# Both tail blocks' second feed-forward matrix as seven block products

## The chip, the cores and the metric

The program runs on one core of one Trainium2 chip, in one launch. The metric is the device time of the whole program in microseconds (us), the median over the runs of one kernel. All data are float32.

## The reference, cut to what matters

The program computes a first block of two layers and then a second block of two layers on 256 tokens of width 1024. The change touches only the feed-forward part of the second block, which runs twice, once in each of its layers (called `A.` and `B.` in the kernel):

```python
ALPHA = (2 * DEPTH) ** 0.25          # DEPTH = 2; the residual is scaled by it

def sq_relu_mlp(x, w1, w2):          # x 256x1024, w1 1024x4096, w2 4096x1024
    return jnp.square(jax.nn.relu(x @ w1)) @ w2

x = layer_norm(ALPHA * x + sq_relu_mlp(x, mlp_w1[i], mlp_w2[i]), ln_ffn_g[i], ln_ffn_b[i])
```

The hidden activations are non-negative and 256x4096; the second product sums over 4096.

## The kernel before, in words

**Digits.** A float32 product is made of three single-pass products. Each operand is split into a high part (`hi`, a copy rounded to the type fp32r, made by ScalarE) and a low part (`lo`, the operand less its high part, made by VectorE), and TensorE sums `lo*hi + hi*lo + hi*hi` (`products`, line 562). A matmul whose operands are plain float32 is called native here.

**Tiles and ring.** Weights come in 2 MB tiles through a ring of three buffers. SyncE issues the load of the next tile into a buffer when TensorE has finished the tile that lay in it (`tile_used`, line 1886; TensorE signals it with the first matmul behind the tile, `tile_done` and `pay`, lines 484 and 458). The low part of a tile is written in place, over the tile (`w_lo`, line 330); the high part goes to two places of 2048 columns, `w_hi_tmp`/`w_hi_rows` and `w_hi_work`/`w_hi_big` in turn. The order of a block's tiles is ff1.0, ff1.1, ff2.0, ff1.2, ff2.1, ff1.3, ff2.2, ... ff1.7, ff2.6, ff2.7 (`_mlp_tiles`, line 117). So tile ff2.n lies in the buffer in which ff1.n lay, and ff1.(n+2) in the buffer of ff2.(n-1).

**The loop.** One turn of the loop is `ff1(n)` and `ff2(n-1)` (lines 621 and 668). `ff1(n)` makes 512 hidden columns as two units (f = 2n and 2n+1), each 48 matmuls of 256 columns into one of PSUM's banks 0 and 1 in turn. `ff2(n-1)` adds 512 rows of the second matrix to the output in banks 4 to 7: 48 matmuls of 512 columns. ScalarE (`act_mlp`, line 1140) and VectorE (`dve_mlp`, line 1167) follow in a fixed order written out by hand: ScalarE copies the high parts of the next tile and makes each unit's relu, square and high part (lines 1151, 1153, 1155), VectorE the low parts (lines 1107 and 1177). Every engine runs its instructions strictly in program order. Behind `ff2(7)` VectorE adds `ALPHA * x` (`add_mlp`, line 2601) and makes the layer norm.

A unit may start when its bank has been read (`wide_.saved`): with two banks this is the unit two before it.

Of the kernel before, what the change touches and what calls it, by code (L numbers as in the profile page):

```python
# [7 lines left out]
F32 = mybir.dt.float32  # L8
F32R = mybir.dt.float32r
ALU = mybir.AluOpType  # L10
ACT = mybir.ActivationFunctionType
# [136 lines left out]
SPLITS2 = ["sbo0", "sbo1"] + _mlp_tiles("A.") + ["dso0", "dso1"] + _mlp_tiles("B.")  # L148


def _places(splits):

    pairs = (("work", "big"), ("tmp", "rows"))
    late = {"in0": ("work", "zb"), "in1": ("tmp", "rows"), "in2": ("work", "scr"), "in3": ("tmp", "rows"),
            "in4": ("hT", "work"), "in5": ("z0", "big"), "in6": ("scr", "zb"), "in7": ("work", "hT"),
            "in8": ("zb", "scr"), "in9": ("work", "hT"), "in10": ("zb", "hT"),
            "up_nsa": ("mid", "tmp"), "up_ret": ("scr", "hT"),
            "out0": ("work", "zb"), "out1": ("mid", "tmp"),
            "gate0": ("tab0", "big"), "gate1": ("tmp", "rows"),
            "dso0": ("big", "big_a"), "dso1": ("big_b", "work")}  # L160
# [5 lines left out]
    places.update((name, mixed[name]) for name in splits if name in mixed)  # L166
    return places


# [104 lines left out]
def program(nc, ctx, I, out):  # L274
# [39 lines left out]
    def hid_slot(f):  # L314

        return f % (4 * HID_SLOTS)
# [13 lines left out]
    w_lo = [digits(f"w_lo{i}", f"ring{i}", 0, SLOT) for i in range(RING)]  # L330
    rows_t = rows[:, :].rearrange("p (t n) -> p t n", t=TT)

    gate_t = scr[:, 0:TT * D].rearrange("p (t n) -> p t n", t=TT)

    def part(lo, width, pattern=None, **sizes):
# [118 lines left out]
    def pe_kit(pe, st, wide_, aux_, tiles, splits, places):  # L454
# [134 lines left out]
        def mlp(pre, turns, between=None, second_token=None, between_at=3, last_turn=None):  # L589
# [31 lines left out]
            def ff1(n):  # L621
# [43 lines left out]
                            some(q, u, range(KT))  # L665
                tile_done()

            def ff2(n):
                lo, hi = next_split(f"{pre}ff2.{n}", 4, D)
                wait_split(f"{pre}ff2.{n}", 1)  # L670
                pe.wait_ge(hid_lo_ready.sem, st.at(hid_lo_ready, FB // 2 * mlp_nth(pre) + 2 * n + 2))
                for q in range(4):
                    t, c = divmod(q, 2)
                    for k in range(4):
                        last = n == 7 and k == 3
                        if n == 7 and q == between_at and k == 2 and between:
# [418 lines left out]
    def lower_split(st, eng, tiles, splits, name):  # L1095

        for h in range(2):
            lower_half(st, eng, tiles, splits, name, h)

    def lower_half(st, eng, tiles, splits, name, h):  # L1100

        n, nth = tiles.index(name), splits.index(name)
        signal, _ = lower_digits(name, splits)
        places, width = PLACES if splits is SPLITS else PLACES2, split_halves(name)
        c = slice(h * width, (h + 1) * width)
        eng.wait_ge(w_hi_ready.sem, st.at(w_hi_ready, 2 * nth + h + 1))
        eng.tensor_tensor(w_lo[n % RING][:, c], ring[n % RING][:, c], w_hi[places[name][h]][:, 0:width].bitcast(F32), ALU.subtract) \  # L1107
            .then_inc(st.up(signal), 1)

    def hidden_pairs(name):  # L1110

# [12 lines left out]
    def act_mlp_by_token(st, act, wide_, pre, tiles, splits, halves):  # L1124

        def save_rows(t):
            b, nth = wide_.next(f"{pre}f{t}")
            act.wait_ge(wide_.ready.sem, st.at(wide_.ready, nth))
            act.activation(hid_rows[t], b, ACT.Copy).then_inc(st.up(wide_.saved), 1)

        act_split(st, act, tiles, splits, f"{pre}ff1.1", halves)
        save_rows(0)
        save_rows(1)
        act_split(st, act, tiles, splits, f"{pre}ff2.0")
# [3 lines left out]
        act_mlp(st, act, wide_, pre, tiles, splits, 1)  # L1138

    def act_mlp(st, act, wide_, pre, tiles, splits, done=0):  # L1140

# [15 lines left out]
    def dve_mlp_by_token(st, dve, pre, tiles, splits):  # L1157

        lower_split(st, dve, tiles, splits, f"{pre}ff1.1")
        lower_split(st, dve, tiles, splits, f"{pre}ff2.0")  # L1160
# [1401 lines left out]
    def dve_tail(dve, st, head):  # L2562
        wide_, aux_ = wide.again(WIDE2), head.aux

        def tt(o, a, b, op):
            return dve.tensor_tensor(o, a, b, op)  # L2566
# [4 lines left out]
        def stt(o, a, s1, b, op0, op1):  # L2571
            return dve.scalar_tensor_tensor(out=o, in0=a, scalar=s1, in1=b, op0=op0, op1=op1)  # L2572
# [28 lines left out]
        def add_mlp(first, t, c):  # L2601
            n = 2 * t + c
            dve.wait_ge(ff2_ready.sem, st.at(ff2_ready, first + n + 1))
            xv = x[:, t, c * BANK:(c + 1) * BANK]
            stt(xv, xv, ALPHA, scores[:, n * BANK:(n + 1) * BANK], ALU.mult, ALU.add).then_inc(st.up(ff2_saved), 1)

        def layer_norm(n, add, between=None, turned_first=None):

# [559 lines left out]
```

## Time and profile before

| What | Value |
|---|---|
| median of 3 runs (lowest, highest) | 1469.02 us (1468.73, 1470.3) |
| span of the profiled execution | 1467.4 us |
| median less that span (what lies around it) | 1.6 us |
| PE busy | 1442.2 us, 98% of the span |
| DVE busy | 814.0 us, 55% |
| ACT busy | 730.8 us, 50% |
| DMA queue q1, share of 16 engines | 48.1% |

PE is TensorE's matmuls, PEld its weight loads, DVE VectorE, ACT ScalarE, SPq the queue of SyncE that issues the weight loads. The profile is of one execution; of its own time only the span, from the first instruction to the last, is shown, and the runs' median is 1.6 us above it. The loop of block A is at 1000.6 to 1171 us of the span, that of block B at 1290.4 to 1460 us. A matmul's duration in a row includes its way through the array, so neighbouring matmuls overlap: what one costs in a dense stretch is the distance of the starts.

### The profile page before, as it was taken

Reading aid. Unit: us, or ns where it says so; the run is one execution under the profiler, and the core shown is the slowest. Engines: PE = TensorE matmul, PEld = TensorE weight load, DVE = VectorE, ACT = ScalarE, POOL = GpSimd, SP = SyncE. Lnnn points to the kernel's source line nnn. Section 1 sums busy time; section 2 is a strip of 40 time slices with the busy share of each in tenths; the row PEclk is TensorE's granted clock in tenths of the full one; section 3 lists DMA queues with packets and bytes.
Section 4 is the critical chain, followed back from the end, with each engine's and each line's share of the span. In section 5 each row is a group of like instructions: output and inputs, shape, how many; then the busy total and the mean of one; then the engine's idle time right before and its main releaser. Section 6 shows DMA issues by size and latency. Waiting matters only on the chain.

```text
span 1467.4 us, 19978 instructions
## 1 busy us (share of the span) xinstructions
PE 1442.2 (98%) x8640; PEld 1231.4 (84%) x8640; DVE 814.0 (55%) x1010; ACT 730.8 (50%) x910; POOL 289.6 (20%) x109
## 2 busy tenths in 40 slices
PE   7999999999999999999999999999999999999998
PEld 5788889988877788888989788688998888888986
DVE  5337665454553364854444669875444557554445
ACT  4465635544455554654455366646544336264452
POOL 4598150000029694410000000000000004000000
PEclk9999999999999999999999999999999999999999
DMA  8833345654446543445566353215654453255451
GB/s 302 297 124 128 125 146 198 213 211 180 173 153 236 196 146 116 166 170 210 173 198 219 122 190 115 98 61 183 230 187 172 153 196 115 74 206 209 172 198 60
DMA packets 121222, 250.26 MB, mean 171 GB/s; under 512 B 15040, under 2 KB 27056, under 8 KB 121008
## 3 DMA queue, kind: packets, MB, share of 16 engines
q1 hardware_dynamic: 120872, 248.90, 48.1%
q8 instruction: 68, 1.11, 0.3%
q14 instruction: 18, 0.15, 0.0%
q10 hardware_dynamic: 264, 0.10, 0.0%
HBM read 247.94 MB, written 1.05 MB: 170 GB/s over the span
## 4 chain that ended last, share of the span: by engine, by line
PE 93%; DVE 4%; POOL 1%; issue 1%; ACT 1%; DMA 0%; DVEq 0%
PE psum L464 90%; PE psum L471 4%; DVE x L2572 1%; POOL w_lo L1107 1%; DVE big L2566 1%; DMA work<-in_norm_mix 0%; DVE rows L1379 0%; DVE w_lo L1107 0%; DVE tiny L2615 0%; DVE big L2572 0%; DVE ht_lo L1353 0%; DVE hT L1348 0%; DVE pT L2816 0%; DVE rows L2566 0%; DVE ht_lo L2566 0%
## 5 line engine op out<-in xcount | busy, mean ns | idle before, releaser
L464 PE MATMUL psum<-ht_hi,w_lo 128*128 128x256 f32 x960 | 269.2, 281 | 0.9 <-issue 0.6
L464 PE MATMUL psum<-w_lo,ht_hi 128*128 128x512 f32 (+1 forms) x576 | 222.5, 390 | 0.9 <-DVE w_lo L1107 0.9
L464 PE MATMUL psum<-w_lo,hid_hi 128*128 128x512 f32 x512 | 202.4, 395 | 0.0
L464 PEld LDWEIGHTS psum<-ht_hi,w_lo 128*128 128x128 f32 x960 | 179.7, 187 | 3.2 <-issue 2.0
L1087 ACT ACTIVATE w_hi_work<-ring 128x2048 fp32r<-128x2048 f32 x40 | 76.5, 1913 | 153.2 <-PE psum L464 150.5
L1107 DVE TENSOR_TENSOR w_lo<-ring,w_hi_work 128x2048 fp32r<-128x2048 f32 x29 | 66.5, 2292 | 129.9 <-ACT w_hi_work L1087 129.9
L1177 DVE TENSOR_TENSOR hid_lo<-work,hid_hi 128x512 fp32r<-128x512 f32 x60 | 41.5, 692 | 160.4 <-ACT hid_hi L1155 160.4
L464 PEld LDWEIGHTS psum<-w_lo,ht_hi 128*128 128x128 f32 x576 | 108.5, 189 | 22.5 <-DVE w_lo L1107 1.7
L464 PE MATMUL psum<-ht_lo,w_hi_rows 128*128 128x256 f32 x448 | 125.0, 279 | 0.0
L464 PE MATMUL psum<-ht_lo,w_hi_tmp 128*128 128x256 f32 x448 | 125.0, 279 | 0.0
L464 PE MATMUL psum<-ht_hi,w_hi_tmp 128*128 128x256 f32 x448 | 124.9, 279 | 0.0
L464 PE MATMUL psum<-ht_hi,w_hi_rows 128*128 128x256 f32 x448 | 124.4, 278 | 0.0
L464 PEld LDWEIGHTS psum<-w_lo,hid_hi 128*128 128x128 f32 x512 | 96.1, 188 | 21.7
L1107 POOL TENSOR_TENSOR w_lo<-ring,w_hi_work 128x2048 fp32r<-128x2048 f32 x12 | 57.5, 4795 | 255.2 <-ACT w_hi_work L1087 255.2
L1151 ACT ACTIVATE work<-psum 128x512 f32<-128x512 f32 x60 | 35.9, 598 | 142.3 <-PE psum L464 142.3
L1107 DVE TENSOR_TENSOR w_lo<-ring,w_hi_tmp 128x2048 fp32r<-128x2048 f32 x36 | 82.5, 2292 | 40.0 <-ACT w_hi_tmp L1087 40.0
L464 PE MATMUL psum<-hT,ring 128*128 128x256 f32 (+2 forms) x480 | 89.8, 346 | 0.0
L464 PE MATMUL psum<-w_hi_big,hid_lo 128*128 128x512 f32 x224 | 88.9, 397 | 0.0
L464 PE MATMUL psum<-w_hi_big,hid_hi 128*128 128x512 f32 x224 | 88.4, 395 | 0.0
L464 PE MATMUL psum<-w_hi_work,hid_hi 128*128 128x512 f32 x224 | 88.4, 395 | 0.0
L464 PE MATMUL psum<-w_hi_work,hid_lo 128*128 128x512 f32 x224 | 88.2, 394 | 0.0
L464 PEld LDWEIGHTS psum<-hT,ring 128*128 128x128 f32 (+1 forms) x480 | 78.2, 186 | 10.5 <-issue 2.4
(399 smaller groups left out, 3382.9 us busy)
## 6 DMA issues: line engine op xcount, KB each, us to landing
ring<-in_w_ff SPq DMA_DIRECT2D x32, 2048.0 KB, 7.9
ring<-in_mlp_w SPq DMA_DIRECT2D x32, 2048.0 KB, 8.4
ring<-in_w_in SPq DMA_DIRECT2D x19, 2048.0 KB, 8.1
ring<-in_w_out SPq DMA_DIRECT2D x4, 2048.0 KB, 8.1
ring<-in_w_ple_gate SPq DMA_DIRECT2D x4, 2048.0 KB, 8.0
ring<-in_sb_ssm_w_in SPq DMA_DIRECT2D x4, 2048.0 KB, 8.9
ring<-in_dsa_w_in SPq DMA_DIRECT2D x3, 2048.0 KB, 8.7
ring<-in_w_up_nsa SPq DMA_DIRECT2D x2, 2048.0 KB, 8.4
```

Source lines behind the costliest of these rows:

```text
L464: ins = pe.matmul(o, lhsT, rhs, start=start, stop=stop)
L471: ins = pe.transpose(o, in_, ident[0:n, 0:n])
L1087: act.activation(w_hi[place][:, 0:width], ring[n % RING][:, h * width:(h + 1) * width], ACT.Copy) \
L1107: eng.tensor_tensor(w_lo[n % RING][:, c], ring[n % RING][:, c], w_hi[places[name][h]][:, 0:width].bitcast(F32), ALU.subtract) \
L1151: act.activation(h, b, ACT.Relu).then_inc(st.up(wide_.saved), 1)
L1177: dve.tensor_tensor(lo, h, hi.bitcast(F32), ALU.subtract).then_inc(st.up(hid_lo_ready), 1)
L2566: return dve.tensor_tensor(o, a, b, op)
L2572: return dve.scalar_tensor_tensor(out=o, in0=a, scalar=s1, in1=b, op0=op0, op1=op1)
```

## The change

In the tail blocks (`SEVEN = ("A.", "B.")`) `ff2(0)` to `ff2(6)` are replaced. A tile's 256x512 hidden values and 512x1024 weights are cut in two by two blocks: tokens in halves, the 512 summed rows in halves (of each pair of 128 rows the first or the second, `v`), output columns in halves. The eight block products are replaced by seven, of 128 tokens x 256 rows x 512 columns each, with sums of blocks as operands (the scheme with four sums on either side and seven sums behind). Each product has a PSUM bank (1 to 7) of its own over all seven tiles; the units of `ff1` have bank 0 alone. Five products are made by digits (two rows of 128 each, three matmuls: 6 matmuls a tile), two, into banks 2 and 6, natively in float32 (2 matmuls a tile). The sums, their low parts and the last sums into `x` are VectorE's, the high parts ScalarE's. `ff2(7)` stays as it is, but adds onto the products in banks 4 to 6, and onto an empty bank 7 once VectorE has read it; `ALPHA` is applied in `dve_seven_products`, and `add_mlp` only adds. The high parts of ff1.2 to ff1.7 are split by columns (one half per unit) and all use `tmp`/`rows`; those of ff2.0 to ff2.6 use `work`/`big`. The core of the diff:

```diff
+            def ff1_unit(n, q, w):
+                lo, hi = w
+                wait_split(f"{pre}ff1.{n}", q)
+                _, nth = wide_.next(f"{pre}f{2 * n + q}")
+                pe.wait_ge(wide_.saved.sem, st.at(wide_.saved, nth + 1))
+                ... 48 products matmuls into bank[0]
+            def seven_first(n, lo):
+                m, s = seventh(pre, n), 4 * (n % 2)
+                pe.wait_ge(form_hi.sem, st.at(form_hi, DIGIT_FORMS * m + 1))
+                pe.wait_ge(hid_lo_ready.sem, ...2 * n + 2))
+                for o, v in ((bank[4], 1), (bank[1], 0)):
+                    for u in range(2):
+                        f = s + 2 * u + v
+                        mm(o, hid_lo[:, f, 0:P], col_hi[:, u, v, :], n == 0 and u == 0, False)
+                        mm(o, hid_hi[:, f, 0:P], col_hi[:, u, v, :], False, False, ...)
+            def seven_rest(n, lo):
+                pe.wait_ge(form_lo.sem, st.at(form_lo, DIGIT_FORMS * m + 1))
+                ... hid_hi * low columns, 4 matmuls, banks 4 and 1
+                pe.wait_ge(s_low.sem, st.at(s_low, m + 1))
+                pe.wait_ge(form_lo.sem, st.at(form_lo, DIGIT_FORMS * m + 2))
+                by_digits(bank[5], 2, right_hi[:, :, 1, :], w[:, :, 1, BANK:D], False, None)
+                by_digits(bank[7], 0, right_hi[:, :, 0, :], w[:, :, 0, BANK:D], final, form_used)
+                pe.wait_ge(form_lo.sem, st.at(form_lo, DIGIT_FORMS * m + 3))
+                by_digits(bank[3], 1, t_hi[0], t_lo[0], final, form_used)
+                ... bank[2]: s_form(sums_, 3, u) * t_sum[1], native, 2 matmuls
+                ... bank[6]: hid_f[:, s + 2 * u + 1, P:S] * t_sum[2], native, 2 matmuls
-            for n in range(1, 8):
-                ff1(n)
-                ff2(n - 1)
+            ... ff1(1); seven_first(0, lo); seven_rest(0, lo)
+                for n in range(2, LAST + 1):          # LAST = 7
+                    w = next_columns(f"{pre}ff1.{n}")
+                    ff1_unit(n, 0, w)
+                    lo = seven_open(n - 1)
+                    seven_first(n - 1, lo)
+                    ff1_unit(n, 1, w)
+                    tile_done()
+                    seven_rest(n - 1, lo)
+                    tile_done()
             ff2(7)
+    def act_column_forms(st, act, tiles, pre, n):
+        act.wait_ge(tile_in[at % RING].sem, ...)       # tile ff2.n has landed
+        act.activation(col_hi, blocks(ring[at % RING][:, :])[:, :, :, 0:BANK], ACT.Copy)...
+    def act_right_forms(st, act, tiles, pre, n):
+        act.wait_ge(t_summed.sem, st.at(t_summed, 4 * m + 2))
+        act.activation(right_hi, blocks(ring[at % RING][:, :])[:, :, :, BANK:D], ACT.Copy)...
+        act.activation(t_hi[0], t_sum[0], ACT.Copy)...
+    def act_hidden_forms(st, act, pre, n):
+        act.wait_ge(s_summed.sem, ...); act.activation(s_hi[n % 2], s_sum[n % 2][:, 0:S_WIDTH], ACT.Copy)...
+    def act_mlp_seven(...):                            # hidden(f): relu, square, high part of unit f
+        for n in range(2, LAST):
+            hidden(2 * n)
+            act_split(st, act, tiles, splits, f"{pre}ff1.{n + 1}", (0,))
+            act_column_forms(st, act, tiles, pre, n)
+            hidden(2 * n + 1)
+            act_split(st, act, tiles, splits, f"{pre}ff1.{n + 1}", (1,))
+            act_hidden_forms(st, act, pre, n)
+            act_right_forms(st, act, tiles, pre, n)
+        hidden(2 * LAST); act_split(... ff2.7, (0,)); hidden(2 * LAST + 1); act_split(... ff2.7, (1,))
+    def dve_mlp_seven(st, dve, pre, tiles, splits):
+        for n in range(1, LAST):
+            lower_columns(st, dve, tiles, splits, f"{pre}ff1.{n + 1}", 0)   # 128x2048
+            dve_hidden_sums(st, dve, pre, n)           # 4 sums of 128x256
+            dve_hidden_first(st, dve, pre, n)          # 128x512
+            lower_columns(st, dve, tiles, splits, f"{pre}ff1.{n + 1}", 1)   # 128x2048
+            dve_form_sums(st, dve, tiles, pre, n)      # 4 sums of 128x1024, each waits for the last
+            dve_form_lows(st, dve, tiles, pre, n, range(2))                 # 2 of 128x2048
+            dve_hidden_sums_low(st, dve, pre, n)       # 128x768
+            dve_form_lows(st, dve, tiles, pre, n, range(2, DIGIT_FORMS))    # 128x1024
+        ... low parts of ff2.7 and of units 14, 15
+    def dve_seven_products(st, dve, pre):              # behind dve_mlp_seven
+        dve.wait_ge(seven_done.sem, ...)
+        ... 4 scaled sums, 1 copy, 5 sums, all 128x512; the last signals seven_read
             def ff2(n):
                 for q in range(4):
+                    if pre in SEVEN and q == 3:
+                        pe.wait_ge(seven_read.sem, ...)
```

For n = 1 both halves of ff1.2 are split ahead of the hidden sums; for n = 0 the forms stand ahead of the units' relu.

## Rows read from the trace of the kernel before

**Rows 1.** The page: the chain that ended last, by engine.
```profile
PE 93%; DVE 4%; POOL 1%; issue 1%; ACT 1%; DMA 0%; DVEq 0%
```
**Rows 2.** Windows of ff1(3), ff2(2): PE, PEld, DVE, ACT, POOL busy, clock, DMA, GB/s.
```profile
1046.40:1057.80 11.40, 11.40 (x98) 11.36 (x97) 5.18 (x3) 5.58 (x5) 0.00 (x0) 1.00 0.52 185
1057.80:1068.90 11.10, 11.10 (x49) 8.95 (x49) 5.19 (x3) 5.48 (x5) 0.00 (x0) 1.00 0.52 189
```
**Rows 3.** Timeline of PE in that turn (start, us; line; out<-in; shape).
```profile
1046.44 0.28 PE L464 MATMUL psum<-ht_hi,w_lo 128*128 128x256 f32 x1
...
1057.73 0.40 PE L464 MATMUL psum<-w_hi_work,hid_lo 128*128 128x512 f32 x1
...
1068.92 0.28 PE L464 MATMUL psum<-ht_hi,w_lo 128*128 128x256 f32 x1
```
**Rows 4.** Timeline of PE around four native matmuls (8 records).
```profile
403.17 3.59 PE L464 MATMUL psum<-big,pT 128*128 128x512 f32 x8
406.20 0.80 PE L464 MATMUL psum<-w_hi_tab,ht_lo 128*128 128x512 f32 x1
406.84 0.40 PE L464 MATMUL psum<-w_lo,ht_hi 128*128 128x512 f32 x1
```
**Rows 5.** Timeline of SPq, and the load's time from issue to landing.
```profile
1058.16 0.37 SPq L1899 DMA_DIRECT2D ring<-in_mlp_w  x1
...
ring<-in_mlp_w SPq DMA_DIRECT2D x1, 2048.0 KB, 7.8
```
**Rows 6.** Timeline of ACT in that turn (in brackets: idle before, releaser).
```profile
1046.81 1.92 ACT L1087 ACTIVATE w_hi_work<-ring 128x2048 fp32r<-128x2048 f32 x1 [5.83 <-PE psum L464]
1048.63 1.90 ACT L1087 ACTIVATE w_hi_big<-ring 128x2048 fp32r<-128x2048 f32 x1
...
1057.93 0.60 ACT L1151 ACTIVATE work<-psum 128x512 f32<-128x512 f32 x1 [3.72 <-PE psum L464]
...
1059.76 1.90 ACT L1087 ACTIVATE w_hi_tmp<-ring 128x2048 fp32r<-128x2048 f32 x1
```
**Rows 7.** Timeline of DVE in that turn.
```profile
1059.89 0.69 DVE L1177 TENSOR_TENSOR hid_lo<-work,hid_hi 128x512 fp32r<-128x512 f32 x1 [4.96 <-ACT hid_hi L1155]
1061.70 2.29 DVE L1107 TENSOR_TENSOR w_lo<-ring,w_hi_tmp 128x2048 fp32r<-128x2048 f32 x1 [1.11 <-ACT w_hi_tmp L1087]
1063.91 2.28 DVE L1107 TENSOR_TENSOR w_lo<-ring,w_hi_rows 128x2048 fp32r<-128x2048 f32 x1
```
**Rows 8.** Groups by line and shape: busy us, mean ns, idle before.
```profile
L1379 DVE TENSOR_TENSOR big<-big 128x1024 f32<-128x1024 f32 x4 | 4.9, 1220 | 0.1
L2566 DVE TENSOR_TENSOR big<-big 128x256 f32<-128x256 f32 x8 | 3.0, 422 | 0.1
L1287 ACT ACTIVATE big<-big 128x1024 f32<-128x1024 f32 x2 | 2.1, 1040 | 0.0
```
**Rows 9.** Windows around a gap of PE (columns as rows 2), PE's timeline behind it.
```profile
933.10:935.60 2.50, 0.02 (x1) 0.00 (x0) 2.47 (x4) 2.50 (x2) 0.00 (x0) 0.92 0.97 279
935.60:939.00 3.40, 3.20 (x8) 2.15 (x9) 1.16 (x3) 0.43 (x1) 0.00 (x0) 0.55 1.01 384
...
935.80 3.38 PE L464 MATMUL psum<-tmp,const 128*128 128x384 f32 x8 [2.68 <-DVE rows L2566]
```
**Rows 10.** Timeline of PE early in the program.
```profile
20.73 0.63 PE L464 MATMUL psum<-w_hi_work,ht_hi 128*128 128x512 f32 x1
21.16 0.63 PE L464 MATMUL psum<-w_hi_work,ht_lo 128*128 128x512 f32 x1
```
**Rows 11.** Timeline of DVE at the end of block B, last layer norm.
```profile
1454.53 0.69 DVE L2572 SCALAR_TENSOR_TENSOR x<-x,psum 128x512 f32<-128x512 f32 x1 [1.30 <-PE psum L464]
1455.25 0.69 DVE L2615 BATCH_NORM_STATS2 tiny<-x 128x6 f32<-128x512 f32 x1
...
1456.23 2.87 DVE L2572 SCALAR_TENSOR_TENSOR x<-x,tiny,const 128x512 f32<-128x512 f32 x4
...
1462.01 2.87 DVE L2572 SCALAR_TENSOR_TENSOR x<-x,tiny,const 128x512 f32<-128x512 f32 x4
```

More of the change, by code:

```diff
@@ L147, with _seven_tiles, _by_columns @@
 SPLITS = [f"in{c}" for c in range(N_IN)] + ["up_nsa", "up_ret"] + ["out0", "out1"] + _mlp_tiles("") + ["gate0", "gate1"]
-SPLITS2 = ["sbo0", "sbo1"] + _mlp_tiles("A.") + ["dso0", "dso1"] + _mlp_tiles("B.")
+LAST = 7
+SEVEN = ("A.", "B.")
+DIGIT_SUMS = 1
+DIGIT_FORMS = 2 + DIGIT_SUMS
+def _seven_tiles(pre):
+    return [f"{pre}ff2.{n}" for n in range(LAST)] if pre in SEVEN else []
+def _by_columns(name):
+    pre, _, kind = name.rpartition("ff1.")
+    return pre in SEVEN and kind.isdigit() and int(kind) >= 2
+SPLITS2 = ["sbo0", "sbo1"] + [n for n in _mlp_tiles("A.") if n not in _seven_tiles("A.")]
+SPLITS2 += ["dso0", "dso1"] + [n for n in _mlp_tiles("B.") if n not in _seven_tiles("B.")]
 def _places(splits):
@@ L166, in _places @@
     places.update((name, mixed[name]) for name in splits if name in mixed)
+    for pre in SEVEN:
+        if f"{pre}ff1.0" in splits:
+            places.update((f"{pre}ff1.{n}", pairs[1]) for n in range(1, LAST + 1))
+            places.update((name, pairs[0]) for name in _seven_tiles(pre))
+            places[f"{pre}ff2.{LAST}"] = pairs[1]
     return places
@@ L666, in ff1 @@
                 tile_done()
+            def ff1_unit(n, q, w):
[4 more added lines that the diff above has]
+                for u in range(2):
+                    c = slice((2 * q + u) * P, (2 * q + u + 1) * P)
+                    for k in range(KT):
+                        last = k == KT - 1
+                        products(bank[0][:, u * S:(u + 1) * S], hi(k, c), lo[:, k, c], ht_hi[:, k, :], ht_lo[:, k, :],
+                                 k == 0, last, wide_.ready if last and u == 1 else None)
@@ L688, in mlp @@
                 ff1(0)
-            for n in range(1, 8):
-                ff1(n)
-                ff2(n - 1)
+            if pre in SEVEN:
+                ff1(1)
+                lo = seven_open(0)
+                seven_first(0, lo)
+                seven_rest(0, lo)
+                tile_done()
[7 more added lines that the diff above has]
+                    seven_rest(n - 1, lo)
+                    tile_done()
+            else:
+                for n in range(1, 8):
+                    ff1(n)
+                    ff2(n - 1)
             ff2(7)
@@ new lines, in act_right_forms @@
+    def act_right_forms(st, act, tiles, pre, n):
+        at, m = tiles.index(f"{pre}ff2.{n}"), seventh(pre, n)
+        form_free(st, act, tiles, pre, n, 2)
+        act.wait_ge(t_summed.sem, st.at(t_summed, 4 * m + 2))
+        act.activation(right_hi, blocks(ring[at % RING][:, :])[:, :, :, BANK:D], ACT.Copy).then_inc(st.up(form_hi), 1)
+        act.activation(t_hi[0], t_sum[0], ACT.Copy).then_inc(st.up(form_hi), 1)
+        if DIGIT_SUMS > 1:
+            act.wait_ge(t_summed.sem, st.at(t_summed, 4 * m + 3))
+            act.activation(t_hi[1], t_sum[1], ACT.Copy).then_inc(st.up(form_hi), 1)
@@ new lines, in act_hidden_forms, with act_mlp_seven, hidden @@
+    def act_hidden_forms(st, act, pre, n):
+        act.wait_ge(s_summed.sem, st.at(s_summed, seventh(pre, n) + 1))
+        act.activation(s_hi[n % 2], s_sum[n % 2][:, 0:S_WIDTH], ACT.Copy).then_inc(st.up(s_high), 1)
+    def act_mlp_seven(st, act, wide_, pre, tiles, splits):
+        def hidden(f):
+            turn, nth = wide_.next(f"{pre}f{f}")
+            b = turn if f < 4 else bank[0]
+            act.wait_ge(wide_.ready.sem, st.at(wide_.ready, nth))
+            at = hid_slot(2 * f)
+            hi, h = (v[:, at:at + 2, :].rearrange("p f t -> p (f t)") for v in (hid_hi, hid_f))
+            act.activation(h, b, ACT.Relu).then_inc(st.up(wide_.saved), 1)
+            act.wait_ge(st.last.sem, st.reached())
+            act.activation(h, h, ACT.Square).then_inc(st.up(act_step), 1)
+            act.wait_ge(st.last.sem, st.reached())
+            act.activation(hi, h, ACT.Copy).then_inc(st.up(hid_hi_ready), 1)
+        hidden(2)
+        act_hidden_forms(st, act, pre, 0)
+        hidden(3)
+        act_split(st, act, tiles, splits, f"{pre}ff1.2")
+        act_column_forms(st, act, tiles, pre, 1)
+        act_hidden_forms(st, act, pre, 1)
+        act_right_forms(st, act, tiles, pre, 1)
+        for n in range(2, LAST):
[6 more added lines that the diff above has]
+            act_right_forms(st, act, tiles, pre, n)
+        hidden(2 * LAST)
+        act_split(st, act, tiles, splits, f"{pre}ff2.{LAST}", (0,))
+        hidden(2 * LAST + 1)
+        act_split(st, act, tiles, splits, f"{pre}ff2.{LAST}", (1,))
@@ new lines, in dve_form_sums @@
+    def dve_form_sums(st, dve, tiles, pre, n):
+        at = tiles.index(f"{pre}ff2.{n}")
+        w = blocks(ring[at % RING][:, :])
+        b11, b12, b21, b22 = (w[:, :, v, c * BANK:(c + 1) * BANK] for v in range(2) for c in range(2))
+        sums_ = ((t_sum[0], b22, b12), (b12, b12, b11), (t_sum[1], b22, b12), (t_sum[2], b21, t_sum[1]))
+        dve.wait_ge(tile_in[at % RING].sem, st.at(tile_in[at % RING], 16 * (at // RING + 1)))
+        for (o, a, b), nth in zip(sums_, (3, None, 4, 5)):
+            if nth:
+                form_free(st, dve, tiles, pre, n, nth)
+            dve.tensor_tensor(o, a, b, ALU.subtract).then_inc(st.up(t_summed), 1)
+            dve.wait_ge(st.last.sem, st.reached())
@@ new lines, in dve_form_lows @@
+    def dve_form_lows(st, dve, tiles, pre, n, which):
+        at, m = tiles.index(f"{pre}ff2.{n}"), seventh(pre, n)
+        w, lo = blocks(ring[at % RING][:, :]), blocks(w_lo[at % RING][:, :])
+        forms = [(lo[:, :, :, 0:BANK], w[:, :, :, 0:BANK], col_hi), (lo[:, :, :, BANK:D], w[:, :, :, BANK:D], right_hi)]
+        forms += [(t_lo[i], t_sum[i], t_hi[i]) for i in range(DIGIT_SUMS)]
+        for i in which:
+            low, v, hi = forms[i]
+            dve.wait_ge(form_hi.sem, st.at(form_hi, DIGIT_FORMS * m + i + 1))
+            dve.tensor_tensor(low, v, hi.bitcast(F32), ALU.subtract).then_inc(st.up(form_lo), 1)
@@ L1133, in act_mlp_by_token @@
         save_rows(1)
-        act_split(st, act, tiles, splits, f"{pre}ff2.0")
+        if pre in SEVEN:
+            act_column_forms(st, act, tiles, pre, 0)
+            act_right_forms(st, act, tiles, pre, 0)
+        else:
+            act_split(st, act, tiles, splits, f"{pre}ff2.0")
         for t in range(TT):
```

161 lines of the change are left out of this document (156 added, 5 removed).

## The prediction, made before the change was run

> **What bounds the kernel now.** First the chain that ended last: TensorE makes up 93% of it [rows 1], so the span is a stream of matmuls, and only what lengthens, shortens or interrupts this stream counts. Then the windows of one turn of the loop: PE is busy for all of both, at the full clock, while DVE works 10.4 and ACT 11.1 of 22.5 us [rows 2]. PE's timeline gives the price of the work by the distance of starts [rows 3]: ff1(n), 96 matmuls of 256 columns, takes 1057.73 - 1046.44 = 11.29 us (0.118 each), ff2(n-1), 48 of 512 columns, 1068.92 - 1057.73 = 11.19 us (0.233 each); a turn takes 22.48 us. Last the timelines of ACT, DVE and SPq in this turn, for how far behind TensorE the other engines run: the load of ff2.3 is issued 0.43 us after ff1(3) ends and lands 7.8 us later [rows 3, 5], and yet nobody waits for it, since ACT's next copy waits for TensorE alone, 5.83 us [rows 6]. That is the slack which the change spends.
>
> **TensorE's own work.** A tile of ff2.0 to ff2.6 had 48 matmuls. Now it has 5 x 6 = 30 by digits, 30 x 0.233 = 6.99 us, and 4 native ones. Four native 128x512 matmuls (8 records) begin at 403.17; the second single-pass matmul behind them begins at 406.84, less one distance 0.233 is 406.61, so 3.44 us in all, 0.86 each [rows 4]. Together 10.43 us for 11.19: 0.76 saved a tile, 10.6 us over 14 tiles, if nobody waits. A turn has 21.72 us of work for TensorE.
>
> **Who waits.** Four things in the code form a loop. (1) ff2.n is loaded into the buffer of ff1.n, so not before unit 2n+1 is done. This is as before. (2) ScalarE now has `act_column_forms(n)`, which waits for that landing, ahead of `hidden(2n+1)`. Queued behind the waiting copy are the relu of unit 2n+1 and all else of ScalarE. (3) The units have bank 0 alone, so unit 2n+2 waits for the relu of unit 2n+1, and unit 2n+3 for that of 2n+2; before, each had one unit of slack. (4) ScalarE reaches `hidden(2n+2)` only behind `act_right_forms(n)`, which waits for VectorE's second form sum, and VectorE comes to that only behind the hidden sums, which need unit 2n+1's high part. So from the end of unit 2n+1 to the end of unit 2n+3, one turn later:
> - to the issue 0.43, landing 7.8 [rows 3, 5];
> - column copy, 2048 wide: start to start 1.82 [rows 6];
> - relu, square, high part, to DVE's start: 1057.93 to 1059.89, 1.96 [rows 6, 7];
> - four hidden sums of 256, each about 0.42 and 0.02 for its wait: 1.76 [rows 8];
> - low part of 512: 0.69, less the 0.08 by which two of DVE overlap (2.29 long, starts 2.21 apart): 0.61; low columns of ff1.(n+1): 2.21 [rows 7];
> - two form sums of 1024: 1.22 each, with the wait between them 2.5 [rows 8];
> - ScalarE's right half 1.82 [rows 6], `t_hi` 1.04 less the overlap, 0.96 [rows 8], relu 0.60 and its signal 0.05 [rows 6];
> - unit 2n+3, 48 x 0.118 = 5.65 [rows 3].
>
> The sum is 28.17; for the hand-overs left out I add 0.1 and take 28.3 us. The rest of DVE's turn (two more form sums, low parts of 2048 twice, 1024 and 768, 2048 for the next tile) fits in beside this: all of DVE's is about 18.7 us, all of ACT's about 13.3. TensorE idles 28.3 - 21.7 = 6.6 us a turn: ahead of unit 2n+2, since the relu of 2n+1 has read bank 0 only 0.43 + 7.8 + 1.82 + 0.65 = 10.7 us after the unit and `seven_rest` lasts 8.57, 2.1 us; ahead of unit 2n+3 4.4 us. A turn costs 28.3 - 22.48 = 5.8 us more. This holds for unit 5 to unit 15, five turns: +29.1 us a block.
>
> **The ends of each block.** From unit 3 to unit 5 no landing is in the way yet (ScalarE has relu 3 ahead of the column copy of ff2.1), but two `seven_first` lie in this turn: 10.43 + 5.65 + 1.86 + 5.65 = 23.6, and the hidden sums and their low part stand between the second token's hidden values and TensorE, where one low part of 0.7 stood; I take 1.0 for it, so 24.6 for 22.48, +2.1. Behind unit 15 the landing of ff2.7 (8.23), a split (1.82), relu, square and high part of unit 15 (1.84, three of ACT back to back), the second split (1.90) and its low part (2.33) end at 16.1 us, while `seven_rest(6)` covers 8.6: TensorE idles 7.5 us. Then VectorE makes ten sums of 512 for the products, each priced as the 0.69 of its low part [rows 7], 7.0, to 23.1, and two tokens' adds and norm: four of 0.72, an aggregation of 0.25, 2.87 for the norm, 6.0 each [rows 11], to 35.1. The fourth quarter of ff2(7) starts at 16.1 + 8.4 = 24.5, after `seven_read`, and ends at 27.3, so VectorE is last here. Before, the second quarter ended at about 1454.4 [rows 11], so unit 15 at 1454.4 - 5.6 - 11.2 = 1437.6, and VectorE at 1462.01 + 2.87 = 1464.9: 27.3 us. So +7.8. In block A the first token's norm, for which the next stage waits, is late by the same.
>
> **The clock.** Where PE idled 2.68 us, the granted clock fell to 0.5 at about the gap's end and stayed there for (0.08 x 2.5 + 0.45 x 3.4) / 0.5 = 3.5 us [rows 9]: 1.2 for 2.4 GHz. At that level starts of 512-column matmuls are 0.43 us apart [rows 10] against 0.233, so a fall costs at most 3.5 x (1 - 0.233/0.43) = 1.6 us, and less where part of it lies in the gap. The new 4.4 us gap stands right ahead of a unit that is on the loop's path. From nothing to 1.6, I take 1.2, being nearest to that row: five turns, two blocks, 12 us. A fall behind the 2.1 us gap would only eat into the 4.4 us gap, and one behind the 7.5 us gap is covered by VectorE.
>
> The Trainium skill says the same against this change: by TensorE: Matmul & The Clock Gate, "Loop structure matters more than you think", a long DMA wait between bursts of matmuls makes each burst start cold. By that rule the clock is paid for in every turn; were it not so, the sum would lack its 12 us. The one mid-kernel gap of this trace agrees.
>
> **The sum.** A block: 2.1 + 29.1 + 7.8 = 39.0; two: 78; clock 12; together +90. The profiled execution's span of 1467.4 becomes 1557.4; the runs' median lay 1.6 above the span, so 1559 us.
>
> **The rivals.**
> - *The clock stays up.* Same loop without the 12 us: 1547. For it: only one gap in the trace shows a fall in mid-kernel, and weight loads and short bursts go on in each turn. Against it: 4.4 us is longer than that gap. 20%.
> - *The clock stays down.* If the three gaps of a turn's work leave the clock low for most of it, both units (11.3) and part of the tile run at 0.43 for 0.233; the 4.4 us slack ahead of the odd unit then covers the even one, and the odd unit on the path costs up to 4.8 instead of 1.2: 10 x 3.6 = 36 more, 1595; half of that, 1577, where it comes and goes. 10%.
> - *Less waiting than the loop says.* A transfer is hidden better than I see (landing earlier in the turn, or the form sums ready before the relu): 25 us a turn, 33 less, 1526. 6%.
> - *Faster: the arithmetic alone counts.* One mechanism: TensorE's stream stays dense, because the waits of ScalarE's queue end inside `seven_rest` and `seven_first`. The price is then -10.6 us, 1458 us. It decides where the loop above takes under 21.7 us, 6.6 less than worked out; 100% PE in the windows of before, 5.83 us of ACT's slack and a landing that nobody awaits speak for it; against it, that the landing alone (8.23) and the relu behind it outlast the 8.57 us of `seven_rest`, whatever the rest costs. 4%.
>
> My forecast has the other 60%. The 8-in-10 range takes in the first rival and half of the second: 1536 to 1582, which is also the forecast with 27.2 to 31.8 us a turn (clock and all) where I take 29.5. A change of under 0.2%, 3 us, can't be told from none here; faster by more 4%, within it 1%, slower 95%.
>
> **What would show it.** In the windows of the loop PE is busy about 0.77 and a turn lasts 28 to 30 us. ACT's column copy (`w_hi_work<-ring`) is released by the DMA of `in_mlp_w`, its right copy (`w_hi_big<-ring`) by DVE, DVE's hidden sums by ACT, and PE's first matmul of each unit by ACT's relu. Ahead of ff2(7) PE waits some 7.5 us for a low part. The clock falls about once a turn. Native matmuls cost 0.86. I am wrong if the column copy doesn't end a wait for the landing, or if PE's gaps sum to under 4 us a turn.

## The result and the profile after

The changed kernel takes 1544.85 us, median of 4 runs (1542.31 to 1546.61); the kernel before, on the same chip, 1468.88 (1467.16 to 1470.3). The ratio is 1.0522, 95% interval 1.0507 to 1.0537: 76 us slower. The forecast was 1559, range 1536 to 1582. In later series some executions of several kernels, the one before included, are 13 to 16 us longer by one wait in the first block, which no kernel here changes (last section); they widen some intervals, and where such a kernel is compared, the median of the other executions stands beside it.

| | before | after |
|---|---|---|
| span of the profiled execution | 1467.4 us | 1544.0 us |
| PE busy | 1442.2 (98%) | 1457.6 (94%) |
| DVE busy | 814.0 (55%) | 933.0 (60%) |
| ACT busy | 730.8 (50%) | 753.5 (49%) |

The chain that ended last, by engine and by line, which answers to [rows 1]:

```profile
PE 77%; DVE 9%; ACT 6%; DMA 5%; issue 1%; POOL 1%; DVEq 0%; ACTq 0%
```

PE made up 93% of it, and DMA, ACT and DVE together 5%. Now those three hold 20%: the chain leaves TensorE once a turn. The waits between 1000 and 1250 us, block A (us in total, times, longest), name the hand-overs:

```profile
ACT w_hi_work L1282 <- DMA ring<-in_mlp_w: 62.8, 6, 13.2
DVE work L1364 <- ACT hid_hi L1312: 56.9, 5, 12.3
PEld psum L515 <- issue: 49.1, 64, 4.5
PE psum L515 <- ACT work L1308: 29.3, 10, 4.1
ACT w_hi_big L1289 <- DVE ring L1344: 25.4, 6, 4.6
```

L1282 is the column copy (the high part of a ff2 tile's left columns), L1308 the relu, L1364 the first hidden sum, L1289 the right copy (the high part of its right columns), L1344 the form sums (of a tile's blocks). All but the third line (TensorE's weight loads, idle with its matmuls) are the four releases that the prediction named. The ring of them can be read once round. PE's timeline, from one odd unit to the next:

```profile
1090.05 0.36 PE L515 MATMUL psum<-ht_hi,w_lo 128*128 128x256 f32 x1 [2.59 <-ACT work L1308]
...
1095.78 1.10 PE L515 MATMUL psum<-w_lo,hid_hi 128*128 128x512 f32 x4
...
1106.63 0.36 PE L515 MATMUL psum<-ht_hi,w_lo 128*128 128x256 f32 x1 [2.11 <-ACT work L1308]
...
1118.49 0.36 PE L515 MATMUL psum<-ht_hi,w_lo 128*128 128x256 f32 x1 [4.12 <-ACT work L1308]
```

The same stretch in the chain of waits (start, us, what; where two instructions overlap, a start is up to 0.1 us later than in a timeline):

```profile
1090.05 6.14 PE psum L515 x49
...
1096.20 7.87 DMA ring<-in_mlp_w
...
1104.09 1.91 ACT w_hi_work L1282
1106.00 0.49 ACT work L1308
...
1107.18 0.64 ACT hid_hi L1312
...
1107.85 0.42 DVE work L1364
...
1110.23 2.28 DVE w_lo L1262
1112.51 1.15 DVE big L1344
...
1113.68 1.24 DVE ring L1344
```

and ACT's timeline where the chain comes back to it:

```profile
1104.09 1.91 ACT L1282 ACTIVATE w_hi_work<-ring 128x2048 fp32r<-128x2048 f32 x1 [11.06 <-DMA ring<-in_mlp_w]
...
1115.00 1.91 ACT L1289 ACTIVATE w_hi_big<-ring 128x2048 fp32r<-128x2048 f32 x1 [4.59 <-DVE ring L1344]
1116.82 1.04 ACT L1290 ACTIVATE t_hi<-big 128x1024 fp32r<-128x1024 f32 x1
```

The odd unit is done at 1095.78 (the matmuls of `seven_rest` start), load issued at 1096.20, landed after 7.87 us, column copy from 1104.09, relu at 1105.91, hidden sums from 1107.85, low columns from 1110.23, form sums from 1112.43, right copy from 1115.00, `t_hi`, relu, and the next odd unit at 1118.49. From odd unit to odd unit (1090.05 to 1118.49) that is 28.44 us; the prediction's sum was 28.17, taken as 28.3.

The clock comes on top. Windows (columns as [rows 2]; the clock is the third column from the end) of a unit behind a 2.11 us gap and of the start of one behind a 4.12 us gap:

```profile
1106.60:1112.40 5.80, 5.77 (x49) 5.80 (x50) 4.39 (x6) 3.78 (x4) 0.00 (x0) 1.00 0.76 243
1118.40:1122.40 4.00, 3.91 (x21) 3.94 (x22) 4.00 (x3) 3.04 (x3) 0.00 (x0) 0.62 0.00 0
```

The second unit lasts from 1118.49 to 1125.74, 7.25 us, where the one at 1090.05 took 5.73: this fall to half, 1.2 GHz, costs 1.5 us. The right copy (L1289) starts at 1027.1 for n = 1 and at 1175.6 for n = 6, so five turns last 148.5 us, 29.7 each; in block B (1356.94 to 1503.24) 29.3. The prediction had 29.5 with the clock.

### The profile page after: what moved, and what is told of

Read it like the earlier page. It is cut to its first block, busy times and chain, and to the rows that moved or that the text cites. A ratio compares the mean times of both kernels' runs of the same rounds, so it can differ in the third digit from the quotient of the medians.

```text
span 1544.0 us, 19971 instructions
## 1 busy us (share of the span) xinstructions
PE 1457.6 (94%) x8500; PEld 1223.3 (79%) x8500; DVE 933.0 (60%) x1156; ACT 753.5 (49%) x938; POOL 289.3 (19%) x109
## 4 chain that ended last, share of the span: by engine, by line
PE 77%; DVE 9%; ACT 6%; DMA 5%; issue 1%; POOL 1%; DVEq 0%; ACTq 0%
PE psum L515 74%; DMA ring<-in_mlp_w 5%; PE psum L522 3%; DVE w_lo L1262 1%; ACT w_hi_big L1289 1%; ACT w_hi_work L1282 1%; DVE ring L1344 1%; DVE big L1344 1%; DVE x L2916 1%; ACT work L1308 1%; ACT t_hi L1290 1%; POOL w_lo L1255 1%; DVE big L2910 1%; ACT hid_hi L1312 0%; ACT work L1310 0%
## 5 line engine op out<-in xcount | busy, mean ns | idle before, releaser
L515 PE MATMUL psum<-ht_hi,w_lo 128*128 128x256 f32 x960 | 280.1, 292 | 58.1 <-ACT work L1308 57.1
L515 PEld LDWEIGHTS psum<-ht_hi,w_lo 128*128 128x128 f32 x960 | 188.5, 196 | 72.5 <-issue 71.7
L515 PE MATMUL psum<-w_lo,hid_hi 128*128 128x512 f32 x344 | 129.7, 397 | 0.0
L515 PEld LDWEIGHTS psum<-ht_lo,w_hi_rows 128*128 128x128 f32 x448 | 91.7, 205 | 0.1
L515 PEld LDWEIGHTS psum<-ht_hi,w_hi_rows 128*128 128x128 f32 x448 | 90.1, 201 | 0.0
L1255 POOL TENSOR_TENSOR w_lo<-ring,w_hi_big 128x2048 fp32r<-128x2048 f32 x3 | 13.7, 4565 | 401.2 <-DVE work L2910 401.2
L515 PEld LDWEIGHTS psum<-ht_lo,w_hi_tmp 128*128 128x128 f32 x448 | 87.4, 195 | 1.1 <-issue 0.5
L1282 ACT ACTIVATE w_hi_work<-ring 128x2048 fp32r<-128x2048 f32 x14 | 26.7, 1910 | 124.7 <-DMA ring<-in_mlp_w 124.7
L515 PEld LDWEIGHTS psum<-ht_hi,w_hi_tmp 128*128 128x128 f32 x448 | 86.2, 192 | 0.0
L1364 DVE TENSOR_TENSOR work<-work 128x256 f32<-128x256 f32 x14 | 5.9, 424 | 118.6 <-ACT hid_hi L1312 111.7
L515 PEld LDWEIGHTS psum<-w_lo,hid_hi 128*128 128x128 f32 x344 | 63.9, 188 | 14.2 <-issue 0.5
L1521 DVE TENSOR_TENSOR hid_lo<-work,hid_hi 128x512 fp32r<-128x512 f32 x32 | 22.1, 691 | 83.6 <-ACT hid_hi L1495 83.6
```

What stands on the lines that cost most here:

```text
L515: ins = pe.matmul(o, lhsT, rhs, start=start, stop=stop)
L1282: act.activation(col_hi, blocks(ring[at % RING][:, :])[:, :, :, 0:BANK], ACT.Copy).then_inc(st.up(form_hi), 1)
```

## The experiments

Each started from the changed kernel ("after" below) unless it says otherwise. Times are medians; in brackets the ratio to the kernel before, run beside it, with its 95% interval.

**e1: the relu ahead of the column copy.** In `act_mlp_seven`:

```diff
-            act_column_forms(st, act, tiles, pre, n)
             hidden(2 * n + 1)
+            act_column_forms(st, act, tiles, pre, n)
             act_split(st, act, tiles, splits, f"{pre}ff1.{n + 1}", (1,))
```

> ScalarE makes unit 2n+1's relu, square and high part ahead of the column copy that waits for ff2.n's landing; the second half of ff1.(n+1) and all else stay behind that copy. Theory (the loop of four steps): unit 2n+2 no longer waits, but VectorE's form sums still stand behind the low columns of ff1.(n+1), whose high part comes behind the column copy: 8.23 landing, 1.82 and 1.90 two copies of ACT, 2.21 low columns, 2.5 form sums, 1.82 and 0.96 right copy and t_hi, 0.65 relu, 5.65 unit = 25.8 us a turn for 28.3, the gap of about 4 us ahead of the odd unit stays and with it the clock falls. 10 turns: 25 us less than the changed kernel, 1520. Rival 1, only the landing counts and the rest has slack: turns fall to 21.7, near 1467. Rival 2, the copy's place is harmless since the right copy is what sets the turn: no change, 1545.

Measured 1521.68 us (1.0369, 1.0353 to 1.0384). Waits from 1050 to 1180 us, and windows of the start of an odd unit and of the turn before it:

```profile
DVE w_lo L1262 <- ACT w_hi_rows L1225: 36.7, 5, 7.4
PE psum L515 <- ACT work L1308: 19.8, 5, 4.1
```
```profile
1084.10:1087.30 3.20, 3.15 (x15) 3.18 (x16) 3.20 (x2) 3.00 (x3) 0.00 (x0) 0.50 0.02 5
1056.70:1084.10 27.40, 23.49 (x134) 19.90 (x134) 18.11 (x16) 12.73 (x13) 0.00 (x0) 0.94 0.43 154
```

The gap ahead of even units is gone; one of 3.9 to 4.1 us ahead of each odd unit is left, and the clock is at half behind each. A turn is 27.4 us, the 25.8 worked out and 1.6 more, which one fall of the clock (1.5 in the unit above) nearly makes up. The theory holds and both rivals fall: the copy's place costs 2.3 us a turn (29.7 to 27.4), no more, because the form sums still stand behind a half of ff1.(n+1) that is split after the landing: VectorE waits up to 7.4 us for its high part (L1225) ahead of its low columns (L1262).

**e2: the next unit's relu ahead of the right copy.**

```diff
+        hidden(4)
         for n in range(2, LAST):
-            hidden(2 * n)
             ...
             act_hidden_forms(st, act, pre, n)
+            hidden(2 * n + 2)
             act_right_forms(st, act, tiles, pre, n)
-        hidden(2 * LAST)
```

> ScalarE makes unit 2n+2's relu, square and high part ahead of the right copy and t_hi of ff2.n, where it stood behind them; the column copy keeps its place ahead of unit 2n+1's relu. Theory: VectorE's form sums leave the loop, the landing stays: 8.23, 1.82, 0.65, unit 5.65, seven_first 1.86, unit 5.65 = 23.9 us a turn. The 4.4 us gap ahead of odd units goes, the 2.1 us one ahead of even units stays, on the path now. If a gap of 2 us doesn't bring the clock down: 10 turns by 5.6 less than 29.5, 1489; if it does, 1.2 a turn more, 1501. Rival, VectorE's own order sets the turn whatever ScalarE does: over 1535.

Measured 1496.18 us (1.0218, 1.0174 to 1.0261), 1496.0 by the three executions without the long wait. PE's waits from 1055 to 1165 us:

```profile
PE psum L515 <- DVE s_lo L1389: 6.0, 4, 1.9
PE psum L515 <- ACT work L1308: 3.4, 2, 2.0
```

Column copies start at 1060.2 (n = 2) and 1157.9 (n = 6): 24.4 us a turn for the 23.9 worked out. Three of these turns are 24.0 to 24.2, one, behind a fall of the clock at 1079, is 25.6. So the time lies between my two prices, 1489 and 1501, since the clock fell behind some gaps near 2 us and not behind others. What I had not put down: the gap is mostly not ahead of the even unit but inside `seven_rest`, where PE waits for the hidden sums' low part (`s_lo`). It hardly costs more, as turns of 24.0 to 24.2 for 23.9 say: by the sum, the relu would have held the next unit for the same 2 us.

**e3: the relu and the half of ff1.(n+1) ahead of the column copy.**

```diff
-            act_column_forms(st, act, tiles, pre, n)
             hidden(2 * n + 1)
             act_split(st, act, tiles, splits, f"{pre}ff1.{n + 1}", (1,))
+            act_column_forms(st, act, tiles, pre, n)
```

> ScalarE makes unit 2n+1's relu, square and high part and the second half of ff1.(n+1) ahead of the column copy that waits for the landing. Theory: hidden sums and low columns are done (6.5 us behind the unit) before the tile lands (8.23), form sums 10.7, right copy and t_hi 13.8, unit 2n+2 ends at 14.2 and its relu is not late. Nothing in the loop outlasts TensorE's own 21.7 us a turn; no gaps, no clock falls: 10 turns by 7.8 less, 1467. Rival 1, the clock falls come from something else than the gaps: 1467 + 12 = 1479. Rival 2, my 21.7 is short, since the native products or the fourth product wait for VectorE's form sums and low parts inside seven_rest: over 1480, with PE waiting for DVE there.

Measured 1464.18 us (0.9976, 0.9965 to 0.9987). The window from the right copy of n = 1 to that of n = 6:

```profile
1026.40:1134.80 108.40, 108.40 (x671) 92.04 (x670) 90.56 (x76) 64.45 (x60) 0.00 (x0) 1.00 0.57 203
```

Five turns in 108.4 us, 21.7 each, as TensorE's own work says; PE without a gap, the clock at 1.00. Two moved lines take 80 us off, and the kernel is 0.24% faster than the one before, clear of noise but small. The column copy still waits for the landing, 4.2 to 4.5 us a turn, but nothing that the chain needs in that time is queued behind it. Both rivals fall: in the loop no clock falls without the gaps, and PE waits for no low part. From the end of unit 5 to that of unit 15 the ten turns of both blocks last 217.3 us for 224.9 before, 7.6 less; the turn from unit 3 to unit 5 still lasts 24.35 for 22.49 in each block, 3.7 more. The balance of 3.9 less is near the 2.9 by which its time lies below the kernel before (1464.2 for 1467.1).

**e5: the load of ff2.7 made late.** In `sp_tail`, for `A.ff2.7` and `B.ff2.7` alone:

```diff
-            sp.wait_ge(tile_used.sem, where.value(tile_used, n + 1))
+            late = name in ("A.ff2.7", "B.ff2.7")
+            sp.wait_ge(tile_used.sem, where.value(tile_used, n + 2 if late else n + 1))
```

> The load of ff2.7 waits for one tile more (ff1.7), as my prediction had it. Theory: in the changed kernel ff2.7 lies in the buffer of ff2.5 and had landed before unit 15 was done, so the 7.5 us of waiting that I put ahead of ff2(7) never was; made to wait here, it should appear in both blocks: ff2(7) starts 16.1 us behind unit 15 instead of 8.2, and each block's last norm ends 35.1 us behind unit 15 for 26.6 to 29.3 now, 14 us in all: 1559, my forecast. Rival, the end of a block is set by VectorE's ten sums and norms alone, or the landing hides: under 1550.

Measured 1558.77 us (1.0622, 1.0606 to 1.0638), 13.9 above after. PE's timeline at the start of ff2(7) in block A:

```profile
1199.65 0.77 PE L515 MATMUL psum<-w_hi_tmp,hid_lo 128*128 128x512 f32 x1 [7.62 <-DVE w_lo L1255]
```

The wait that I had forecast for the changed kernel, 7.5 us for a low part, is here and 7.62 long. In the changed kernel it doesn't exist. The time is that of my forecast; that they meet to 0.2 us is luck, since other terms were off by some us (next section).

**e8: the gap filled.** 24 matmuls of `ht_hi` with itself, added into bank 7 where they falsify a product, between `seven_first` and the odd unit:

```diff
                     seven_first(n - 1, lo)
+                    for k in range(24):
+                        mm(bank[7][:, 0:S], ht_hi[:, k % KT, 0:P], ht_hi[:, k % KT, :], False, False)
                     ff1_unit(n, 1, w)
```

> The changed kernel with 24 more matmuls of 256 columns (2.8 us), nobody's input, ahead of each odd unit from 5 to 15, in the gap of 4.1 us in which TensorE waits for the relu; they add products into bank 7 that don't belong there. Theory: the turn stays 28.3 us by the loop, the longest gap becomes some 1.5 us, the clock no longer falls behind it, and the 1.2 to 1.6 us a turn that the falls cost go: 1545 less 12, 1533. Rival 1, the clock falls for another reason (the load of a tile, the smaller gap ahead of the even unit): 1545. Rival 2, TensorE's gap is no slack, and the matmuls lengthen the path: 1545 + 10 to 28.

Measured 1536.99 us (1.0455, 1.0374 to 1.0537), 1534.9 by three of four. The window of four turns, from the column copy of n = 2 to that of n = 6:

```profile
1047.90:1161.60 113.70, 101.19 (x632) 86.64 (x632) 72.06 (x60) 50.64 (x48) 0.00 (x0) 0.98 0.41 148
```

A turn is 28.4 us, the bare loop, where after has 29.7: 2.8 us of work added a turn, and each turn 1.3 shorter. No odd unit, ahead of which the gap is now at most 1.3 us, has a fall any more, so those falls come from the long gap. The total gains 8 to 10 us for the 12 put down: unit 5 of each block had no gap to hide the filler (its turn, from column copy to column copy, is 27.0 for 23.9 in block A and 25.4 for 22.7 in block B), and at five of the ten gaps ahead of even units, these five of 1.9 to 2.2 us, the clock still fell.

**e4: block A alone.** `SEVEN = ("A.",)`. Block B then has the old products, but its last add leaves out the factor `ALPHA` on the residual.

> The changed kernel with the seven products in block A alone; block B is as before. Theory: the cost is one block's loop, and nothing carries over from A to B: block A's last norm is 39 us late as in the changed kernel, block B runs as before, 1468 + 39 = 1507. Rival: part of the cost is outside the two loops (a clock that stays down, loads shifted against the rest of the program), so that half the change costs clearly more or less than half of 76: under 1500 or over 1515.

Measured 1506.13 us (1.0226, 1.0159 to 1.0292), from 1501.0 to 1510.6: 37.9 above the kernel before at 1468.2 (without the long wait), half of 76, with a scatter of some 5 us to either side. It fits two separate loops, and the rival (under 1500 or over 1515) falls.

**e6, on top of e3: six products by digits.** `DIGIT_SUMS = 2`.

> On top of e3 (no waits in the loop) the sixth product, into bank 2, is made by digits too: 6 matmuls of 0.233 us for 2 native ones of 0.86, 1.40 for 1.72, 0.32 us a tile; ScalarE gets a copy of 1.0 us and VectorE a low part of 1.2 us a tile more. Theory: with the loop free, TensorE's own work sets the turn, 21.4 us for 21.7, and 14 tiles save 4.5: 1460. Rival 1, VectorE's 1.2 us more lies on the path inside seven_rest: PE waits there for a low part, and the time is that of e3 or above it, 1464 to 1475. Rival 2, a native matmul costs no more than three single-pass ones (0.70): 1464.

Measured 1462.64 us (0.9921, 0.9881 to 0.9961); without the long wait 1462.4 for 1468.2 before, so 5.8 below it where e3 was 2.9. Four turns from the column copy of n = 2:

```profile
1061.50:1147.20 85.70, 85.70 (x546) 75.27 (x544) 78.03 (x64) 55.60 (x52) 0.00 (x0) 1.00 0.55 197
```

21.43 us a turn; e3's same four turns (1045.20 to 1132.27) are 21.77 each. 0.34 saved, 0.32 expected, which sets a native matmul at 0.86 or 0.87, not 0.70. But the gain is 2.9 (1.8 if the two times themselves are compared), not 4.5: the turn from the end of unit 3 to that of unit 5 grew from 24.35 to 25.4 us in each block. PE waits there for a relu, which it doesn't in e3:

```profile
PE psum L515 <- ACT work L1308: 0.8, 1, 0.8
```

So a relu of ScalarE's comes late there; that its extra copy is what delays it is argued, not tested. Half a miss.

**e7, on top of e3: early sums.** In `dve_seven_products`:

```diff
-        dve.wait_ge(seven_done.sem, st.at(seven_done, mlp_nth(pre) + 1))
+        used = 4 * seventh(pre, LAST - 1)
+        dve.wait_ge(form_used.sem, st.at(form_used, used + 2))   # bank 7 (and 1) done
         ...
+        dve.tensor_copy(y_sum, bank[1])...                       # moved up, ahead of the next wait
+        dve.wait_ge(form_used.sem, st.at(form_used, used + 3))   # ahead of the sum with bank 3
         ...
+        dve.wait_ge(form_used.sem, st.at(form_used, used + 4))   # ahead of the sum with bank 2
```

> On top of e3 the sums behind the seven products each wait only for the product that they read, where all waited for the last product, which they don't read. Theory: VectorE's 2.5 us of waiting for PE at the end of each block goes, and the norms come 2.3 us sooner in both blocks, until the last quarter of ff2(7) sets them: 1464.2 less 4.6, 1459.6. Rival, the norm waits for ff2(7) anyway: 1464, VectorE's wait only moves to its first add behind ff2(7).

Measured 1460.18 us (0.9948, 0.9909 to 0.9988); without the long wait 1459.7 for 1468.2, 8.5 below where e3 was 2.9: 5.6 gained, 4.6 expected. VectorE at the end of block A, first e3, then e7:

```profile
1149.54 2.29 DVE L1255 TENSOR_TENSOR w_lo<-ring,w_hi_rows 128x2048 fp32r<-128x2048 f32 x1 [1.11 <-ACT w_hi_rows L1235]
1154.35 2.48 DVE L1423 SCALAR_TENSOR_TENSOR x<-x,psum 128x512 f32<-128x512 f32 x4 [2.52 <-PE psum L515]
```
```profile
1147.19 2.29 DVE L1255 TENSOR_TENSOR w_lo<-ring,w_hi_rows 128x2048 fp32r<-128x2048 f32 x1 [1.11 <-ACT w_hi_rows L1235]
1149.40 1.87 DVE L1423 SCALAR_TENSOR_TENSOR x<-x,psum 128x512 f32<-128x512 f32 x3
```

The 2.52 us wait is gone.

**e9: e3, e6 and e7 together.**

> The order of ScalarE of e3, six products by digits of e6 and the early sums of e7 together. Theory: the three are on different stretches, so the gains add: 1464.2 less 4.5 less 4.6, 1455. Rival, VectorE at some 20 us of a 21.4 us turn is near its own bound and falls behind, and the sum is less than 5 us.

Measured 1457.86 us (0.9917, 0.9877 to 0.9957); without the long wait 1456.6 for 1468.2, 11.6 below the kernel before, where the parts sum to 2.9 + 2.9 + 5.6 = 11.4. It is the best version here, 0.8% faster than the kernel before, and the rival of VectorE at its bound falls. Its PE is busy for 98% of the span, as before the change: nearly all that is left is TensorE's own stream.

## Why the prediction was right, and where not

**The mechanism** was right, step by step: the four releases stand in the waits of the profile after, and undoing them one at a time gave the turns that the sum gives without them: 27.4 for 25.8 and a fall of the clock (e1), 24.0 to 24.2 for 23.9 (e2), 21.7 for 21.7 (e3). The step that mattered most is (2): from n = 2 on a wait of 11 to 13 us ahead of everything else in ScalarE's queue. Before, ScalarE's copies waited for TensorE and not for a landing [rows 6]; the transfer took 7.8 us then [rows 5] and 7.9 now. Only what stood behind it changed.

**TensorE's own work** was right. The timeline of PE in block A's last tile, four native matmuls and what follows:

```profile
1192.26 3.60 PE L515 MATMUL psum<-big,work 128*128 128x512 f32 x8
1195.29 0.80 PE L515 MATMUL psum<-w_hi_tmp,hid_lo 128*128 128x512 f32 x1
1195.93 0.40 PE L515 MATMUL psum<-w_lo,hid_hi 128*128 128x512 f32 x1
```

Read as [rows 4] were: 1195.93 - 0.233 - 1192.26 = 3.44, 0.86 each. The gain of 0.76 a tile is real and shows as soon as nobody waits (e3).

**The turns** were right. From the end of one odd unit to the end of the next, the bounds of the sum (in block A 1037.65, 1067.56, 1095.78, 1125.74, 1156.48, 1187.11), three of the ten turns last 28.2 to 28.4 us (28.3 forecast): in them the odd unit runs at the full clock. In the other seven, 29.8 to 30.7, 30.2 on average, the clock falls at the odd unit, in or behind a gap of 4.12 us. All ten last 296.7 us for 224.9 before, 71.8 more; forecast 10 x (5.8 + 1.2) = 70.

**The clock** holds two errors that nearly cancel, which is luck: ten falls at 1.2 us were put down, seven at 1.9 were paid. There are ten, one a turn. But three came at the gap of 1.9 to 2.2 us ahead of the even unit (block A's at 1078.2): they make that unit slower, so that the gap ahead of the odd one is 2.6 us for 4.1, and no fall came there. So they are free, as the prediction said of such a fall. The price is higher than 1.2: four paid falls hold the clock at half for some 3.4 us, as in [rows 9], and make their turn 1.5 to 1.7 us longer than 28.3, since they lie almost wholly inside the odd unit. The other three (two of them in block A) hold it for some 6.8 us and cost 2.2 to 2.4. One of these starts inside the gap ahead of the unit at 1148.54 and ends in that unit at 1153.4:

```profile
1146.50:1147.00 0.50, 0.00 (x0) 0.00 (x0) 0.50 (x1) 0.50 (x2) 0.00 (x0) 0.65 0.00 0
...
1152.50:1153.00 0.50, 0.50 (x5) 0.50 (x4) 0.50 (x2) 0.00 (x0) 0.00 (x0) 0.50 0.00 0
```

By the page that the prediction drew on, the Trainium skill's TensorE: Matmul & The Clock Gate, "Loop structure matters more than you think", a long wait for a transfer ahead of matmuls makes TensorE run them at its lower clock. The trace agrees in direction, in seven of ten odd units. e8 shows that the price goes with the long gap, 1.3 us a turn over block A's last four.

**The signs.** The four releases and the price of a native matmul came as named. PE is busy for 0.80 of block A's five turns (120.1 of 149.4 us) and 0.81 of block B's (119.5 of 147.3) for the 0.77 named, since its gaps sum to 5.9 and 5.6 us a turn for 6.6: the falls in even units take from them, and matmuls at half clock count as busy. The wait of 7.5 us ahead of ff2(7) did not come.

**The rival "the clock stays up"** (1547) lies nearer to the measured 1544.85 than the forecast does. By the number alone it would have won; the trace rules it out, since the clock is at half in every turn. The number is near for another reason, the next term. **The rival "the clock stays down"** fell: outside these ten stretches the clock was at full speed in both loops.

**The ends of each block** hold the mis-sized term: +7.8 us forecast for each, about 0 measured. SP's, ACT's and PE's timelines at the end of block A:

```profile
1167.64 0.37 SPq L2243 DMA_DIRECT2D ring<-in_mlp_w  x1
```
```profile
1180.19 1.90 ACT L1235 ACTIVATE w_hi_tmp<-ring 128x2048 fp32r<-128x2048 f32 x1
1187.31 0.60 ACT L1308 ACTIVATE work<-psum 128x512 f32<-128x512 f32 x1 [5.22 <-PE psum L515]
...
1189.14 1.90 ACT L1235 ACTIVATE w_hi_rows<-ring 128x2048 fp32r<-128x2048 f32 x1
```
```profile
1187.11 1.10 PE L515 MATMUL psum<-w_lo,hid_hi 128*128 128x512 f32 x4
```

The load of ff2.7 is issued at 1167.64, 19.5 us before unit 15 is done at 1187.11, and its first half is copied at 1180.19 without a wait. The sum has it issued 0.43 us behind unit 15, by the rule that ff2.n lies in the buffer of ff1.n, which also stands in the description of the kernel before. That holds for n from 1 to 6 only. The order of tiles ends ..., ff2.5, ff1.7, ff2.6, ff2.7: three back from ff2.7 is ff2.5, not ff1.7. So `seven_rest(6)` and ff2(7) follow each other with no gap, VectorE's ten sums run beside ff2(7), and its last norm ends at 1541.56 in block B, 26.8 us behind unit 15 (1514.75), where it was 27.3 before [rows 11] and 35.1 forecast. In block A it is 29.2 for 28.8. e5 shows it: give the load the release that I had in mind, and both the 7.5 us wait and the 1559 us appear.

The balance of the profiled span, by the sum's own bounds (ends of units): +76.6, of it turns 71.8 (forecast 70), the turns from unit 3 to unit 5 3.7 (24.35 for 22.49 in each block; forecast 4.2), ends 0.0 (forecast 15.6), and 1.1 that I did not place (forecast nothing). So but for the ends the forecast would have been 1543, for 1544.85 measured.

**Less waiting** (1526) and **faster** (1458) fell as forecasts, but e3 meets the second one's condition, a loop that fits in 21.7 us, and PE's stream is dense there. It takes 1464 and not 1458, since the turns from unit 3 to unit 5 still cost 3.7 us; e9 reaches 1458 by two more changes.

## What to carry to other kernels

An algorithm with fewer matmuls pays only while TensorE's stream stays dense: here the loop cost 5.8 us a turn, without the clock, where the arithmetic saved 0.76. Add up, in program order, the whole ring from one release to the same release a turn later, with every engine's queue that it crosses, and compare it with TensorE's work per turn. Where the ring is longer, look first for a wait on a transfer that stands ahead of short work which somebody needs: here two lines moved past such a wait gave back 80 us, where the change had cost 76. And work out which buffer a tile reuses from the list of tiles, for the last ones by themselves: a rule that holds inside a loop fails at its ends.

## What of the hardware was not expected

- A fall of the granted clock behind a gap is not sure near 2 us: of the ten gaps of 1.9 to 2.2 us ahead of even units in the changed kernel three had a fall at them, of the three of 2.6 us none, of those of 3.9 to 4.2 us (the changed kernel and e1, both blocks) all seventeen. A fall can also lengthen a unit so far that the next gap closes to 2.6 us and no fall follows.
- Extra matmuls that the computation doesn't need made the loop faster (e8, 29.7 to 28.4 us a turn).
- In some executions of several kernels TensorE waits once in the first block, around 546 to 559 us. PE's waits from 541 to 560 us in such an execution (e2); the profiles of executions without those 13 us don't have it, and e6's has it at the same length:

```profile
PE psum L522 <- POOL w_lo L1255: 13.0, 1, 13.0
```

POOL's work itself was not slower there, so the releaser named may not be the cause. It stays open.
